# The lead-in of the mixer: key copies by DMA, second unit's queries in the values' bank, casts on ScalarE

## The reference

```python
# gated linear attention, 8 heads, forward and backward, chunks of 64
A = einsum('bhid,bhjd,bhijd->bhij', qc, kc, decay)
o = einsum('bhid,bhde->bhie', qc * exp(b), S) + einsum('bhij,bhje->bhie', A, vc)
S = exp(b_last)[..., None] * S + einsum('bhjd,bhje->bhde', kc * exp(b_last - b), vc)
# windowed attention, 8 query heads over 2 key heads, 512 cached keys, a sink logit per head
s_loc = where(|qpos - kpos| <= 128, q @ kb * scale, NEG_INF)
s_ctx = q @ kc * scale
p = softmax(concat([s_loc, s_ctx, sink]))[..., :-1]
o = p[..., :span] @ vb + p[..., span:] @ vc
```

## Time and profile before

| | us |
|---|---|
| median of 3 runs | 1649.64 (1649.09 to 1650.05) |
| profiled execution | 1650.88 |
| its span | 1649.1 |
| PE busy in it | 1591.7 |

### The profile page before, as it was taken

The page is one execution under the profiler, slowest core; times in us unless marked ns, Lnnn a source line. Parts: engine busy times, 40 slices in busy tenths (PEclk is TensorE's granted clock), DMA queues, the critical chain, the costliest instruction groups (busy, mean ns, idle before and its releaser), DMA issues.

```text
span 1649.1 us, 31938 instructions
## 1 busy us (share of the span) xinstructions
PE 1591.7 (97%) x11618; PEld 1392.7 (84%) x11618; DVE 974.8 (59%) x1505; ACT 682.9 (41%) x1205; POOL 1023.7 (62%) x786
## 2 busy tenths in 40 slices
PE   4999999998999999999899999999999999999998
PEld 1999778897788877788789898998979899998987
DVE  2813564774665676356866657566694545545458
ACT  2513323323454566213544444444535444444441
POOL 1711455574585799103678777687898767676673
PEclk9999999999899999999999999999999999999999
DMA  8344555749655664334743131332334132231313
GB/s 317 112 130 168 183 183 191 264 143 254 180 174 168 220 186 121 139 126 156 228 167 96 57 102 53 99 89 64 100 129 155 52 102 69 83 102 51 102 52 115
DMA packets 211450, 225.93 MB, mean 137 GB/s; under 512 B 52752, under 2 KB 171664, under 8 KB 208144
## 3 DMA queue, kind: packets, MB, share of 16 engines
q1 hardware_dynamic: 209248, 224.46, 42.7%
q10 hardware_dynamic: 2096, 0.02, 0.1%
HBM read 177.22 MB, written 47.24 MB: 136 GB/s over the span
## 4 chain that ended last, share of the span: by engine, by line
PE 44%; POOL 4%; DVE 1%; issue 1%; ACT 0%; DMA 0%; SPq 0%; DVEq 0%; ACTq 0%; POOLq 0%
PE ff_banks L3169 8%; PE ff_banks L3170 8%; PE ff_banks L3171 8%; PE ff_banks L3144 7%; PE ff_banks L3142 7%; PE ff_banks L3143 7%; POOL h_whi L2815 1%; POOL h_xop L2412 1%; POOL h_wlo L2827 1%; POOL h_whi L2822 1%; DVE ff_tmp L3016 0%; DMA ff_hb<-in_w_ff 0%; DVE ff_acc L3006 0%; DVE ff_acc L2973 0%; POOL h_wlo L2862 0%
## 5 line engine op out<-in xcount | busy, mean ns | idle before, releaser
L3142 PE MATMUL ff_banks<-h_xop,h_whi 128*128 128x320 f32 x888 | 275.2, 310 | 4.6 <-POOL h_whi L2815 2.0
L3144 PE MATMUL ff_banks<-h_xop,h_whi 128*128 128x320 f32 x888 | 274.4, 309 | 0.0
L3143 PE MATMUL ff_banks<-h_xop,h_whi 128*128 128x320 f32 x888 | 274.3, 309 | 0.0
L2973 DVE TENSOR_TENSOR ff_acc<-ff_acc,ff_banks 128x512 f32<-128x512 f32 x296 | 200.6, 681 | 100.6 <-PE ff_banks L3171 99.0
L3169 PE MATMUL ff_banks<-h_wlo 128*128 128x512 f32 x580 | 226.5, 390 | 1.6 <-DVE ff_acc L2973 0.8
L3171 PE MATMUL ff_banks<-h_wlo 128*128 128x512 f32 x580 | 225.6, 389 | 0.0
L2815 POOL TENSOR_TENSOR h_whi<-mid_raw,h_whi 128x512 fp32r<-128x512 f32 x149 | 207.4, 1408 | 1.4 <-ACT h_whi L2667 1.4
L2827 POOL TENSOR_TENSOR h_wlo<-mid_raw,h_wlo 128x320 fp32r<-128x320 f32 x128 | 116.6, 912 | 127.6 <-ACT mid_raw L2704 127.6
L3142 PEld LDWEIGHTS ff_banks<-h_xop,h_whi 128*128 128x128 f32 x888 | 166.7, 188 | 8.3 <-issue 4.0
L3143 PEld LDWEIGHTS ff_banks<-h_xop,h_whi 128*128 128x128 f32 x888 | 166.7, 188 | 1.1
L3144 PEld LDWEIGHTS ff_banks<-h_xop,h_whi 128*128 128x128 f32 x888 | 166.7, 188 | 0.0
(11 more groups left out here) (320 smaller groups left out, 3782.0 us busy)
## 6 DMA issues: line engine op xcount, KB each, us to landing
mid_raw<-in_w_ff SPq DMA_DIRECT2D x124, 512.0 KB, 4.3
mid_raw<-in_w_ada SPq DMA_DIRECT2D x18, 1024.0 KB, 7.5
early_room<-qk_by_channel SPq DMA_DIRECT2D x20, 512.0 KB, 4.1
proj<-prj_stage SPq DMA_DIRECT2D x60, 152.0 KB, 1.9
mid_raw<-in_w_in SPq DMA_DIRECT2D x6, 1216.0 KB, 7.3
early_room<-in_w_ada SPq DMA_DIRECT2D x6, 1024.0 KB, 10.9
decays<-early_room SPq DMA_DIRECT2D x8, 640.0 KB, 4.4
early_room<-decays SPq DMA_DIRECT2D x20, 256.0 KB, 2.8
```

The costliest lines, as they stand in the source:

```text
L2973: dve.tensor_tensor(acc[:, p, at], acc[:, p, at], down[n % RING], ALU.add).then_inc(added, 1)
L3142: pe.matmul(out, w_hi[:, k], x_hi[:, k], start=(k == 0), stop=False)
L3143: pe.matmul(out, w_hi[:, k], x_lo[:, k], start=False, stop=False)
L3144: mm = pe.matmul(out, w_lo[:, k], x_hi[:, k], start=False, stop=(k == KH - 1))
```

## The change

GpSimd's copies of the keys' high part into kone are replaced by two DMAs on SP, issued between the states' loads and the values'. GpSimd then scales step 2 directly behind step 1 and fills the ones afterwards. queries(1) moves behind queries(0) and into the bank pv, which `values` uses later. ScalarE takes over the sink's scaling and the two mask casts. dve_state(2) is split in kept, new and sum, set at three places; low_queries(1) moves up. raw_context(1,0) goes ahead of pe_scores(3), dve_scores(3) goes from slot 0 into slot 1, and queries(2) goes behind the values of slot 1. GpSimd's pool_mid waits for the mid two steps before.

```diff
@@ Recurrence
     def pool_mid(self, pool, x):
         pool.wait_ge(self.o_ready, x - 1)
+        pool.wait_ge(self.mid_ready, 2 * x - 4)
...
+        self.dve_kept(dve, x)
+        self.dve_new(dve, x)
+        self.dve_sum(dve, x)
@@ Keys
     def pe_ones(self, pe):
-        pe.wait_ge(self.one_ready, self.N)
+        pe.wait_ge(self.one_ready, 16 * KV)
-    def pool(self, pool, n):
-        pool.wait_ge(self.hl_ready, n + 1)
-        pool.tensor_copy(self.keys_of(self.kone, slice(0, DH), n), self.keys_of(self.khl, slice(0, DH), n).bitcast(F32)).then_inc(self.one_ready, 1)
+    def sp_ones(self, sp):
+        sp.wait_ge(self.hl_ready, self.N)
+        for kv in range(KV):
+            sp.dma_start(self.kone[0:DH, kv].bitcast(F32), self.khl[0:DH, kv].bitcast(F32)).then_inc(self.one_ready, 16)
@@ mixer, SP
                 rec.sp_states(sp)
+                keys.sp_ones(sp)
@@ GpSimd
                 projection_stored(pool)
-                for n in range(2):
-                    keys.pool(pool, n)
                 rec.pool_scaled(pool, 1)
+                rec.pool_scaled(pool, 2)
                 pool.wait_ge(filled, 2)
-                pool.wait_ge(keys.one_ready, 2)
-                pool.wait_ge(rec.qe_ready, 2)
+                pool.wait_ge(rec.qe_ready, 3)
                 pool.memset(kone[DH:EX, :, :].bitcast(F32), 1.0).then_inc(filled, 1)
                 pool.wait_ge(filled, 3)
-                rec.pool_scaled(pool, 2)
-                for n in range(2, keys.N):
-                    keys.pool(pool, n)
                 rec.pool_scaled(pool, FIRST)
@@ PE
-            return score[:, 0] if u < LEAD else rec.ps[:, 1]
+            return score[:, 0] if u == 0 else pv[:, :] if u == 1 else rec.ps[:, 1]
...
                 queries(0)
+                queries(1)
                 rec.pe_turned(pe, 1)
...
                 raw_local(0, 1)
-                queries(1)
                 rec.pe_outputs(pe, 2)
...
                         rec.pe_turned(pe, FIRST)
-                        pe.wait_ge(qlow_ready, 2)
+                        raw_context(1, 0)
                         rec.pe_scores(pe, FIRST)
-                        raw_context(1, 0)
...
-                    if w in query_at:
+                    if w > 1 and w in query_at:
                         queries(query_at[w])
...
+                    if w == 1:
+                        queries(query_at[w])
@@ ScalarE
                 rec.act_turned(act, 1)
+                high_queries(1)
+                act.wait_ge(tables_in, 48)
+                act.activation(sink8[:, :], sink[:, :], ACT.Copy, scale=DH ** 0.5).then_inc(tables, 1)
                 rec.act_output(act, 1)
                 rec.act_decays(act, FIRST)
                 rec.act_turned(act, 2)
-                high_queries(1)
+                act.activation(maskb[:, 0, :], maskr[:, 2, :], ACT.Copy).then_inc(tables, 1)
+                act.activation(maskb[:, 1, :], maskr[:, 0, :], ACT.Copy).then_inc(tables, 1)
@@ VectorE
                 rec.dve_mid(dve, 2)
+                rec.dve_kept(dve, 2)
                 rec.dve_scores(dve, 2)
+                low_queries(1)
                 top_context(0, 1)
-                dve.tensor_scalar(sink8[:, :], sink[:, :], DH ** 0.5, None, ALU.mult).then_inc(tables, 1)
                 top_local(0, 1)
                 dve.wait_ge(tables, 3)
                 peaks(0)
-                low_queries(1)
-                rec.dve_state(dve, 2)
+                rec.dve_new(dve, 2)
                 spread(0)
+                rec.dve_sum(dve, 2)
                 top_context(1, 0)
-                dve.tensor_copy(maskb[:, 0, :], maskr[:, 2, :]).then_inc(tables, 1)
-                dve.tensor_copy(maskb[:, 1, :], maskr[:, 0, :]).then_inc(tables, 1)
                 for w in range(SLOTS + 2):
                     ahead((w, 0))
+                    if w == 1:
+                        rec.dve_scores(dve, FIRST)
...
-                    if w in scores_at:
+                    if w and w in scores_at:
                         rec.dve_scores(dve, scores_at[w])
```

More of the change, by code:

```diff
@@ L1406, in dve_state, with dve_kept, dve_sum @@
             return
+        self.dve_kept(dve, x)
+        self.dve_new(dve, x)
+        self.dve_sum(dve, x)
+    def dve_kept(self, dve, x):
+        i, d, t = self.place(x)
+        st = self.state[0 if i < NTP else 1]
         self.wait_state(dve, x - 1)
         dve.tensor_tensor(self.kept[:, :, :], st[:, d], self.decayed(d, t, slice(0, P), 1), ALU.mult).then_inc(self.kept_ready, 1)
-        dve.wait_ge(self.ds_ready, x + 1)
-        dve.tensor_tensor(self.new[:, :, :], self.update(), self.decayed(d, t, slice(0, P), 2), ALU.mult).then_inc(self.new_ready, 1)
+    def dve_sum(self, dve, x):
+        i, d, t = self.place(x)
+        st = self.state[0 if i < NTP else 1]
         dve.wait_ge(self.new_ready, x + 1)
@@ L1593, in mixer @@
         REC_END = 2 * (X - FIRST)
-        LEAD = 1
         finish_at = {done_slot[u] + 1: u for u in range(U)}
@@ L1648, in mixer @@
                 room[1] = [(spread_ready, u + 1)]
-        query_slot = {1: -1, **{u: w for w, u in query_at.items()}}
+        query_slot = {u: w for w, u in query_at.items()}
         def rec_steps(w):
@@ L1826, in queries @@
                     pe.wait_ge(xq_in[n % 2], 32 * (n // 2) + 32)
-                    if u < LEAD:
-                        keys.pe_room_free(pe, 3)
+                    if u < 2:
+                        keys.pe_room_free(pe, 3 - u)
                     else:
```

## The result

The changed kernel is slower: 1651.71 us in the median against 1648.75 for the kernel before beside it, 21 runs each; the ratio is 1.0016, 95% interval [1.0009, 1.0024], that is 2.6 us (1.5 to 4.0). The forecast was 2.4 us faster, with a range that ended at 1649.2.

What follows compares the result with a forecast made beforehand. PE bounds the mixer's steady part; only standing time in the lead-in can be won. 2.1 us at g3 plus 0.27 from turn_peaks(1) make 2.4, so 1649.64 - 2.4 = 1647.2 us, range 1644.8 to 1649.2.

Steps and rivals of the forecast that it cites:

- VectorE's chain: Lead-in: without GpSimd's casts, dve_mid(2) takes 0.41 us per half, dve_scores(2) comes 2.2 us earlier, g0 3.8 us earlier.
- Rival D: Lead-in: dve_mid(2) still stands, behind the memset and ke(3), dve_scores(2) at 411.2; 1648.0 us; chance 0.07.
- The moved queries, the split update, the mask casts: Lead-in and slot 0: queries(1) fits a gap at no cost, dve_sum(2)'s 0.6 us wait is hidden, casts leave VectorE.
- d: SP's queue: time the copies take of the DMA engines, delaying all SP issues behind them; 3.45 us, ends 2.5 and 5.1.
- the stretch into which they are put: Lead-in, 403 to 410 us: its DMA rate, 266 GB/s, was taken for the copies' 917.5 KB, giving 3.45 us.
- Rival B: SP's queue: copies run at half the best rate, 182 GB/s, since half the partitions take part; 1648.7 us; chance 0.24.
- My own sign of being wrong: End of the lead-in: forecast is wrong if decays(4) lands outside 418.5 to 420 us.
- Nothing, at most 0.3: Head of slot 0: PE's pe_ones waits for copies landing about 412.1 (413.5 at the slow end) against 413.2.
- Rival E: decays(4) on SP, then weights(0): copy far slower, gain gone at 5.9 us, each further us lost; chance 0.08.
- the chain of decays(4): SP to ScalarE: decays(4) lands at 419.45, weights(0) ends at 421.75 and releases g2; g3 comes 2.1 us earlier.
- It stays to the end: After the head of slot 2: PE is the bound and nothing in the change acts, so the 2.4 us gain remains.

Runs made afterwards that it cites:

- e1: Changed kernel with the key copies made by ScalarE (seven copies of 64x512) and none issued by SP; ratio to the kernel before 0.9987.
- e14: Second profile of e3, unchanged; profile only, its execution took 1645.93 us.
- e3: e1 plus two DMAs of the copies' 917,504 bytes that nobody reads, spread over 128 partitions; ratio to the kernel before 0.9998.
- e11: Second profile of the changed kernel, unchanged; profile only, slot 2 at 33.5 us from queries(0).
- e2: e1 plus two DMAs of the change's size and shape, 64 partitions x 7168 B, that nobody reads; ratio to the kernel before 1.0005.
- e4: Changed kernel with the load of decays(4) issued ahead of the copies on SP; ratio to the kernel before 1.0016.
- e10: Second profile of e4, unchanged; profile only, its execution took 1653.71 us.

## Why the prediction was wrong

**VectorE's chain: right.** dve_mid(2) beside the memset takes 0.43 us a half, dve_scores(2) is 2.3 us earlier (forecast 2.2), pe_turned(3) and g0 in e1 3.5 and 3.7 (3.5 and 3.8). Rival D is out. The Trainium skill's rule ("SBUF — State Buffer", "Who interferes with whom") now has its other half: 0.43 us beside a memset, 3.07 beside casts.

**The moved queries, the split update, the mask casts: nothing,** as said; e1 has them all and gains. They were not measured one by one.

**The failed step is the size of d,** the time for which the copies hold the queue: 3.45 us, "the stretch into which they are put", with ends 2.5 and 5.1. It measured 7.0 in the usual profiles. Two things were wrong in it. The copies' own packets took 4.8 to 5.0 us of the engines' time, because the rate of that stretch (266 GB/s) doesn't hold for 64 partitions; for 128 it does, 2.8 to 3.2 us in e14 and e3. Rival B's half rate, d = 5.0, was right for this part, and I had its reason at hand and gave it 0.24. And d was taken to be the copies' time alone, while the small packets behind them took another 2.5 to 3.5 us more than without them; no rival had that as a mechanism. The stated range ended at 1649.2, which is d = 5.4 in my terms. My own sign of being wrong came true: decays(4) landed 23.9 us behind queries(0), where 18.2 to 19.7 was allowed. The Trainium skill's figures ("SBUF — State Buffer", section "Door 1: The DMA port swizzle (why [64,N] ≈ [32,N])") give an estimate of 4.7 us for 64 partitions and, at its 328 GB/s, 2.8 for 128. The traces agree for the copies' own packets; what the copies do to the packets behind them was in neither.

**"Nothing, at most 0.3" for PE's wait at pe_ones failed as well, by the same term.** The landing was put at 412.1, 11.8 us behind queries(0), from the 3.2 us of a 128 KB load and the further bytes at the stretch's rate; the copies landed at 16.9 and PE was let go at 17.1. In the changed kernel this was the last wait ahead of g2, by 0.4 us (0.9 in e11). By the ratios, the queue's hold on decays(4) costs 3.0 us (e1 to e2) and PE's wait another 1.8 (e2 to the change), each with some 2 us either way. They are not a sum of independent parts: e4 takes the first away and gains nothing.

**Rival E named the consequence:** decays(4) late, the gain gone at d = 5.9, a us lost per us past that, now also through pe_ones. At 7.0 that gives 1.1 us slower for the chain of decays(4); the changed kernel measured 2.6. PE's wait and the lower clock behind it, which the forecast had priced at nothing, are what the traces show beside that chain; their shares are not told apart. E had 0.08, and its reason, a rate far from any in the rows, was not what happened: the copies' own rate was B's.

**"It stays to the end": right,** the last piece was 1217.1 to 1218.9 us in every kernel.

## What to carry to other kernels

A DMA in a full queue is to be priced by what is issued behind it and who waits for that, and by its own shape: a transfer over 64 partitions took the engines 1.5 to 1.8 times as long here as the same bytes over 128, and slowed the small packets behind it too. If the bytes can't be spread over all partitions, an engine that is idle just then (ScalarE, 0.54 us per 64x512 here) is the better copier. Where two chains of the same transfer end together, taking one away shows nothing; take away the transfer.

## What the runs showed that I had not expected

The 64-partition copies slow down what is behind them by more than their own rate explains: of the 7.0 us about 4.9 are their own packets, the rest are packets of 256 B at 30 to 33 ns instead of about 20. Over 128 partitions there was no such part (19 to 21 ns). SP, an issuing engine, is held up to 5.67 us in one issue of a values' load (e10; 0.64 in the kernel before). And repeated profiles of one kernel put the landing of the same transfer up to 4 us apart, so one profile of such a lead-in doesn't tell its usual length.
